# The output projection of a hybrid decoder layer: two row halves of 512 columns with the sample rows apart, in place of three blocks of 344

## What is computed

```
h = rmsnorm(x, g_mix);  z = h @ w_in
y = concat(dilated attention, banded attention) * silu(gates)
h = x + y @ w_out                                       # the stage that changes
out = rmsnorm(h + (p @ w_ple) * sigmoid(rmsnorm(h, g_ple) @ w_pg), g_final)
```

## Time and profile before

| | |
|---|---|
| median of 3 runs | 2786.28 us (2779.0 to 2786.41) |
| the profiled execution | 2782.93 us |
| its span in the profile | 2780.7 us |
| PE busy | 2574.9 us, 93% |
| DVE, ACT, POOL busy | 31%, 22%, 22% |
| mean granted clock of PE | 0.952 |

### The profile page before, as it was taken

One profiled execution on the slowest core, in us unless ns is written; L12 is line 12 of the kernel. 1 busy time (PEld: TensorE's weight loads), 2 busy tenths in 40 slices (PEclk: granted clock), 3 DMA queues, 4 the chain that ended last, 5 costly groups with the idle time before them and its releaser, 6 DMA issues.

```text
span 2780.7 us, 40810 instructions
## 1 busy us (share of the span) xinstructions
PE 2574.9 (93%) x16857; PEld 2394.1 (86%) x16857; DVE 856.3 (31%) x2130; ACT 610.4 (22%) x1458; POOL 618.7 (22%) x653
## 2 busy tenths in 40 slices
PE   4999999999999999999999988989999959999980
PEld 4998888888888898888888988879999949999980
DVE  7022322322322314444444213141101163233324
ACT  5022222222222213334544100020000030111113
POOL 2322222222222222211222222223333201111110
PEclk7999999999999999999999999899999979999995
DMA  4232222222222224434443343163222262322316
GB/s 165 65 111 86 84 87 85 88 84 88 88 84 88 69 81 117 123 113 136 129 129 113 117 134 97 56 194 92 81 80 84 73 192 84 93 85 83 93 54 240
DMA packets 301818, 287.96 MB, mean 104 GB/s; under 512 B 20721, under 2 KB 267305, under 8 KB 298281
## 3 DMA queue, kind: packets, MB, share of 16 engines
q1 hardware_dynamic: 278754, 241.11, 28.8%
q10 hardware_dynamic: 17856, 27.34, 2.8%
q0 software_dynamic: 5024, 16.92, 1.7%
HBM read 215.48 MB, written 69.81 MB: 103 GB/s over the span
## 4 chain that ended last, share of the span: by engine, by line
PE 84%; DVE 7%; DMA 5%; ACT 2%; issue 1%; POOL 1%; SPq 0%; POOLq 0%; DVEq 0%; ACTq 0%
PE psum L786 18%; PE psum L788 17%; PE psum L787 17%; PE psum L859 5%; PE psum L861 5%; PE psum L860 5%; PE psum L634 4%; PE psum L610 3%; PE psum L620 3%; PE psum L708 2%; PE psum L810 1%; PE psum L664 1%; DMA out<-f_out 1%; PE psum L689 1%; PE psum L675 1%
## 5 line engine op out<-in xcount | busy, mean ns | idle before, releaser
L786 PE MATMUL psum<-act_hi,w_hi 128*128 128x344 f32 x3264 | 1086.0, 333 | 14.4 <-DVE act_lo L1324 13.5
L788 PE MATMUL psum<-act_hi,w_lo 128*128 128x344 f32 x3264 | 1057.9, 324 | 0.0
L787 PE MATMUL psum<-act_lo,w_hi 128*128 128x344 f32 x3264 | 1057.9, 324 | 0.0
L786 PEld LDWEIGHTS psum<-act_hi,w_hi 128*128 128x128 f32 x3264 | 628.4, 193 | 35.4 <-issue 29.6
L787 PEld LDWEIGHTS psum<-act_lo,w_hi 128*128 128x128 f32 x3264 | 626.9, 192 | 0.0
L788 PEld LDWEIGHTS psum<-act_hi,w_lo 128*128 128x128 f32 x3264 | 626.8, 192 | 0.0
L567 POOL CAST w_hi<-w_raw 128x512 fp32r<-128x512 f32 x272 | 179.8, 661 | 1645.1 <-PE psum L788 1505.4
L569 POOL TENSOR_TENSOR w_lo<-w_raw,w_hi 128x512 fp32r<-128x512 f32 x272 | 366.2, 1346 | 21.8
L1135 DVE COPY prob_t<-psum 128x512 f32<-128x512 f32 (+2 forms) x96 | 53.4, 557 | 497.3 <-PE psum L634 490.8
L937 ACT ACTIVATE prob_t<-psum 128x512 f32<-128x512 f32 (+2 forms) x96 | 47.1, 491 | 420.5 <-PE psum L634 388.4
L859 PE MATMUL psum<-act_hi,u_even 128*128 128x344 f32 x384 | 125.7, 327 | 8.6 <-DVE u_even L1347 7.8
(11 more groups left out here) (190 smaller groups left out, 2742.4 us busy)
## 6 DMA issues: line engine op xcount, KB each, us to landing
w_raw<-in_w_in SPq DMA_DIRECT2D x208, 256.0 KB, 3.0
w_raw<-in_w_out SPq DMA_DIRECT2D x64, 256.0 KB, 2.8
u_raw<-in_w_pg SPq DMA_DIRECT2D x16, 1024.0 KB, 6.2
z_scratch<-stage ACTq DMA_DIRECT2D x72, 172.0 KB, 1.9
h_scratch<-h_row ACTq DMA_DIRECT2D x16, 516.0 KB, 3.3
h_stage<-h_scratch SPq DMA_DIRECT2D x16, 516.0 KB, 4.7
h_in<-h_scratch SPq DMA_DIRECT2D x48, 172.0 KB, 2.6
x_in<-in_x_prompt SPq DMA_DIRECT2D x8, 1024.0 KB, 5.3
```

The lines of the kernel that those rows point to most:

```text
L786: pe.matmul(psum[:, bank, 0:T3], w_hi[:, slot, x, :], act_hi[:, k, rows], start=(k == 0), stop=False, skip_group_check=True)
L787: pe.matmul(psum[:, bank, 0:T3], w_hi[:, slot, x, :], act_lo[:, k, rows], start=False, stop=False, skip_group_check=True)
L788: return pe.matmul(psum[:, bank, 0:T3], w_lo[:, slot, x, :], act_hi[:, k, rows], start=False, stop=stop, skip_group_check=True)
```

## The change

The rows of the output projection are cut into two halves of the prompt (512 columns each, a full PSUM bank) and the sample's 8 columns apart. A new tile `ys_both` holds the sample's high and low parts side by side (16 columns per k). For each k TensorE now runs `key_tile`: high weights by high and by low activations of half 0; high weights by all 16 sample columns at once; low weights by the high activations of half 0; low weights by the 8 high sample columns; then the three products of half 1. That is six matmuls of 512 columns, one of 16, one of 8; before, nine of 344. k is outermost for every tile, the wait on `h_bank_free` covers all banks of tile i-2 at once, and the wait on `s_split` comes first. The residual comes in four 128-row pieces for each half and one 8-row piece. x_cols is loaded by two DMAs. ACT copies two banks of 512; DVE adds the two sample parts from PSUM into `h_row` by a reduce, and waits for the store two tiles back before it writes.

```diff
+            ("ones", [P, P], F32), ("y_in", [P, 4, S], F32), ("ys_both", [P, KT, 2 * NB], F32R))
...
-                for t in range(2):
-                    q0 = T3 * t
-                    sp.dma_start(x_cols[:, par, 3 * t:3 * t + 2, :], ...)
-                    sp.dma_start(x_cols[0:88, par, 3 * t + 2, :], ...)
-                sp.dma_start(x_cols[:, par, 6:8, :], ...)
-                sp.dma_start(x_cols[0:80, par, 8, :], ...)
-                sp.dma_start(x_cols[80:88, par, 8, :], x_s[:, cols]) ...
+                sp.dma_start(x_cols[:, par, 0:8, :], x_p[:, cols].rearrange("(c p) n -> p c n", p=P)) ...
+                sp.dma_start(x_cols[0:NB, par, 8, :], x_s[:, cols]) ...
...
+            def key_tile(i, k):
+                slot, x = (WG * (NZ + i) + k // WG) % WRING, k % WG
+                b0, first, last = 3 * (i % 2), k == 0, k == KT - 1
+                hi_w, lo_w = w_hi[:, slot, x, :], w_lo[:, slot, x, :]
+                for t in range(2):
+                    rows = slice(512 * t, 512 * t + 512)
+                    pe.matmul(psum[:, b0 + t, :], hi_w, act_hi[:, k, rows], start=first, ...)
+                    pe.matmul(psum[:, b0 + t, :], hi_w, act_lo[:, k, rows], ...)
+                    if t == 0:
+                        pe.matmul(psum[:, b0 + 2, 0:2 * NB], hi_w, ys_both[:, k, :], start=first, ...)
+                    mm = pe.matmul(psum[:, b0 + t, :], lo_w, act_hi[:, k, rows], ...)
+                    if t == 0:
+                        pe.matmul(psum[:, b0 + 2, 0:NB], lo_w, ys_both[:, k, 0:NB], ...)
+                return mm
...
-            for i in range(1, KT):
-                for t in range(3):
-                    ...
-                    for k in range(KT):
-                        ...
-                        mm = three(bank, NZ + i, k, t, False)
-                    residual(i, t, bank)
+            for i in range(KT):
+                par = i % 2
+                if i >= 2:
+                    pe.wait_ge(sem("h_bank_free"), 3 * (i - 1))
+                for k in range(KT):
+                    if i == 0:
+                        pe.wait_ge(sem("y_split"), k + 1)
+                    if k % WG == 0:
+                        pe.wait_ge(sem("w_split"), WG * (NZ + i) + k // WG + 1)
+                    mm = key_tile(i, k)
+                    ...
+                pe.wait_ge(sem(f"xc_loaded{par}"), 32 * (i // 2 + 1))
+                for t in range(2):
+                    for x in range(4):
+                        mm = pe.matmul(psum[:, 3 * par + t, x * P:(x + 1) * P], x_cols[:, par, 4 * t + x, :], ident[:], ...)
+                    mm.then_inc(sem("h_produced"), 1)
+                pe.matmul(psum[:, 3 * par + 2, 0:NB], x_cols[0:NB, par, 8, :], ident[0:NB, 0:NB], ...).then_inc(sem("h_produced"), 1)
...
-                for t in range(3):
+                for t in range(2):
                     act.wait_ge(sem("h_produced"), 3 * i + t + 1)
-                    act.activation(h_row[:, par, T3 * t:T3 * (t + 1)], psum[:, 3 * par + t, 0:T3], ACT.Copy) ...
+                    act.activation(h_row[:, par, 512 * t:512 * t + 512], psum[:, 3 * par + t, :], ACT.Copy) ...
...
-            chain(dve.tensor_copy(act_hi[:, :, S:R], ystmp[:]))
-            dve.tensor_tensor(act_lo[:, :, S:R], ystmp[:], hi32[:, :, S:R], ALU.subtract) ...
+            chain(dve.tensor_copy(ys_both[:, :, 0:NB], ystmp[:]))
+            dve.tensor_tensor(ys_both[:, :, NB:], ystmp[:], ys_both[:, :, 0:NB].bitcast(F32), ALU.subtract) ...
...
             for i in range(KT):
+                dve.wait_ge(sem("h_produced"), 3 * i + 3)
+                if i >= 2:
+                    dve.wait_ge(sem(f"h_stored{i % 2}"), 16 * (i // 2))
+                both = psum[:, 3 * (i % 2) + 2, 0:2 * NB].rearrange("p (c n) -> p n c", c=2)
+                dve.tensor_reduce(h_row[:, i % 2, S:R], both, AX.X, ALU.add).then_inc(sem("h_bank_free"), 1)
                 dve.wait_ge(sem("h_bank_free"), 3 * i + 3)
```

More of the change, by code:

```diff
@@ L216, in build @@
         ysm = zs[:, 0:KT, :]
-        acc, h_row, sq, x_cols, ones, y_in = at(
+        acc, h_row, sq, x_cols, ones, y_in, ys_both = at(
             W_END, ("acc", [P, R], F32), ("h_row", [P, 2, R], F32), ("sq", [P, R], F32), ("x_cols", [P, 2, 9, P], F32),
-            ("ones", [P, P], F32), ("y_in", [P, 4, S], F32))
+            ("ones", [P, P], F32), ("y_in", [P, 4, S], F32), ("ys_both", [P, KT, 2 * NB], F32R))
         u_even, y_nat, h_in, gcol = at(0, ("u_even", [P, 2, KT + 2, P], F32R), ("y_nat", [P, 2, 3, P], F32), ("h_in", [P, 2, T3], F32),
@@ L481, in load_x_cols @@
                 cols = slice(i * P, i * P + P)
-                for t in range(2):
-                    q0 = T3 * t
[L484 to L488, removed]
+                sp.dma_start(x_cols[:, par, 0:8, :], x_p[:, cols].rearrange("(c p) n -> p c n", p=P)).then_inc(sem(f"xc_loaded{par}"), 16)
+                sp.dma_start(x_cols[0:NB, par, 8, :], x_s[:, cols]).then_inc(sem(f"xc_loaded{par}"), 16)
             sp.wait_ge(sem("ys_ready"), 1)
@@ L804, in _ @@
                         mm.then_inc(sem("w_used"), 1)
[L806 to L811, removed]
+            def key_tile(i, k):
[4 more added lines that the diff above has]
+                    rows = slice(512 * t, 512 * t + 512)
+                    pe.matmul(psum[:, b0 + t, :], hi_w, act_hi[:, k, rows], start=first, stop=False, skip_group_check=True)
+                    pe.matmul(psum[:, b0 + t, :], hi_w, act_lo[:, k, rows], start=False, stop=False, skip_group_check=True)
+                    if t == 0:
+                        pe.matmul(psum[:, b0 + 2, 0:2 * NB], hi_w, ys_both[:, k, :], start=first, stop=False, skip_group_check=True)
+                    mm = pe.matmul(psum[:, b0 + t, :], lo_w, act_hi[:, k, rows], start=False, stop=False, skip_group_check=True)
+                    if t == 0:
+                        pe.matmul(psum[:, b0 + 2, 0:NB], lo_w, ys_both[:, k, 0:NB], start=False, stop=False, skip_group_check=True)
+                return mm
@@ L813, in _ @@
             pe.wait_ge(sem("bank_free"), UNITS)
             pe.wait_ge(sem("ys_ready"), 1)
-            for k in range(KT):
[L816 to L820, removed]
-                for t in range(3):
-                    mm = three(t, NZ, k, t, False)
-                if k % WG == WG - 1 and k < KT - 1:
-                    mm.then_inc(sem("w_used"), 1)
@@ L825, in _ @@
-            for t in range(3):
-                residual(0, t, t)
-            for i in range(1, KT):
[L828 to L834, removed]
-                        mm = three(bank, NZ + i, k, t, False)
-                        if t == 2 and k % WG == WG - 1 and k < KT - 1:
-                            mm.then_inc(sem("w_used"), 1)
-                    residual(i, t, bank)
+            pe.wait_ge(sem("s_split"), 2)
@@ new lines, in _ @@
+            for i in range(KT):
[8 more added lines that the diff above has]
+                    mm = key_tile(i, k)
+                    if k % WG == WG - 1 and k < KT - 1:
+                        mm.then_inc(sem("w_used"), 1)
+                pe.wait_ge(sem(f"xc_loaded{par}"), 32 * (i // 2 + 1))
+                for t in range(2):
+                    for x in range(4):
+                        mm = pe.matmul(psum[:, 3 * par + t, x * P:(x + 1) * P], x_cols[:, par, 4 * t + x, :], ident[:], start=False, stop=(x == 3), skip_group_check=True)
+                    mm.then_inc(sem("h_produced"), 1)
+                pe.matmul(psum[:, 3 * par + 2, 0:NB], x_cols[0:NB, par, 8, :], ident[0:NB, 0:NB], start=False, stop=True, skip_group_check=True).then_inc(sem("h_produced"), 1)
@@ L1041, in _ @@
                     act.wait_ge(sem("h_squared"), i - 1)
-                for t in range(3):
+                for t in range(2):
                     act.wait_ge(sem("h_produced"), 3 * i + t + 1)
-                    act.activation(h_row[:, par, T3 * t:T3 * (t + 1)], psum[:, 3 * par + t, 0:T3], ACT.Copy).then_inc(sem("h_bank_free"), 1)
+                    act.activation(h_row[:, par, 512 * t:512 * t + 512], psum[:, 3 * par + t, :], ACT.Copy).then_inc(sem("h_bank_free"), 1)
                 act.wait_ge(sem("h_bank_free"), 3 * i + 3)
@@ L1319, in _ @@
             dve.wait_ge(sem("produced"), UNITS)
-            chain(dve.tensor_copy(act_hi[:, :, S:R], ystmp[:]))
-            dve.tensor_tensor(act_lo[:, :, S:R], ystmp[:], hi32[:, :, S:R], ALU.subtract).then_inc(sem("s_split"), 2)
+            chain(dve.tensor_copy(ys_both[:, :, 0:NB], ystmp[:]))
+            dve.tensor_tensor(ys_both[:, :, NB:], ystmp[:], ys_both[:, :, 0:NB].bitcast(F32), ALU.subtract).then_inc(sem("s_split"), 2)
             for k in range(KT):
```

## The result

The changed kernel takes **2840.68 us** (median of 4 runs, 2835.63 to 2844.27) against 2785.53 for the kernel before: 1.0202 of it, 95% interval 1.018 to 1.0224. It is slower by 55 us where 41 were forecast, and lies 0.7 us above the range of 2804 to 2840. In a second set of runs (experiment 7) it took 2833.48 (2830.28 to 2840.32), 1.0182 of before (1.015 to 1.0213). That this median lies inside the range says little: the whole moves by some 10 us with what lies outside the stage, and the stage itself was 12 us off in both.

A forecast was written before the change was run, and what follows sets the result against it. The prediction took TensorE's matmul rate to bound the output projection after tile 0. It added 40.8 + 0.2 = +41.0 us to the profiled 2782.9, giving 2823.9 us, range 2804 to 2840.

The forecast's parts named there:

- What bounds the stage: Output projection: for 15 of 16 tiles bound only by TensorE's matmul rate, never idle over 371.1 us, clock 1.00.
- the clock's rival: Output projection: TensorE's granted clock falls to 1.2 GHz for a tenth of the k, +34 us more, 2858; chance 0.06.
- Order and banks: Output projection: k outermost and one wait for all three banks of tile i-2, met some 20 us early; no cost.
- weights, x_cols and the DVE sum: Output projection: POOL's weight split, fewer x_cols DMA issues and DVE's sample sum change nothing, within half a microsecond.
- The small matmul: Output projection, 16 or 8 columns: each costs the uncovered weight load behind it, 110 ns, 220 for each k.
- Both rivals with a hidden load: Load behind a small matmul hidden, 20 ns each: 2761 without long ones' fixed part, chance 0.04; 2780.5 with it, 0.03.
- A 512-column matmul: Output projection's long products: 512 / 2.4 plus a fixed 13.4 ns, 226.7 ns each; six are 1360 ns.
- overhead by column: Long matmuls' excess grows with columns, 233.2 ns for 512: a k of 1619 ns, +50.2 us, 2833.3.
- The old k: Output projection before: nine 344-column matmuls at 156.7 ns, 1410 ns for each k.
- The residual: Residual matmuls of each tile: 18 records cost 2.0 us in either version; change zero, bounds 0.1 us a tile.
- Tile 0: Output projection's first tile: supply-bound, longer k hidden in PE's waits, no backlog, only the last k exposed: +0.2 us.
- 40.8: Output projection, tiles after the first: each k 1580 ns, 170 more than 1410, over 15 x 16 = 240: +40.8 us.

The follow-up runs named there:

- experiment 7: The changed kernel run once more, unaltered: 2833.48 us, 1.0182 of the kernel before.
- experiment 5: The kernel before, still 344 columns, with k outermost for all tiles and one wait for the three banks: 2783.57 us against 2781.5, 1.0006.
- 1: The changed kernel without both small matmuls for k = 1 to 15: 2786.56 us, 1.0016 of the kernel before.
- 9: The kernel before with one 16-column matmul added for each k of tiles 1 to 15, into a spare bank: 2811.92 us, 1.0097 of before.
- 4: The changed kernel with the 16-column matmul moved between the two long ones using the same high weights: 2836.24 us, 1.019 of the kernel before.
- 3: The changed kernel with each small matmul replaced by one of 236 columns for k = 1 to 15: 2835.91 us, 1.0193 of the kernel before.
- experiment 8: The changed kernel with sample columns stationary and weights streaming past, once in four k, for k = 1 to 15: 2815.74 us, 1.0108 of the kernel before.
- experiment 6: The changed kernel with eight runs of single-kind matmuls added twice behind TensorE's last work: 512 columns took 234.0 ns in float32r, 215.7 in bfloat16.
- experiment 2: The changed kernel with the sample's residual matmul on all 128 rows, zero-padded, instead of 8: 2833.79 us, 1.018 of the kernel before.

## Why the prediction was right in kind and short in size
The windows of tiles 1 to 15 hold 240 k and the residuals of 16 tiles less 0.1 to 0.3 us of the last. With 2.01 us for a residual before and 2.29 after (2012.37 - 2010.08, the start of its first matmul, a long step after the load at 2009.85), a k is (371.25 - 31.9) / 240 = 1414 ns before and (424.31 - 36.4) / 240 = 1616 after. The steps between weight loads, averaged over the same windows, give 1414 and 1616 too. That is the check that counts, since the terms below are taken from these windows and would add up to them in part by themselves. By the prediction's own steps:

- **What bounds the stage: right.** TensorE's rate of matmuls alone, before and after; no wait appeared on PE in tiles 1 to 15 and the clock stayed at 1.00 (the clock's rival fell). Order and banks cost nothing (experiment 5); weights, x_cols and the DVE sum left PE waiting nowhere in 424.31 us.
- **The small matmul: right.** Taken at 110 ns, measured 108 in the changed kernel, 111 and 113 by taking out and putting in (experiments 1 and 9). Both rivals with a hidden load are out: a repeat is paid (4), 220 free columns fit under a load (3), and only a shorter load makes it cheaper (8).
The Trainium skill (TensorE: Matmul & The Clock Gate, "Wait — 56ns, not 53.3ns?") has a floor of about 25 ns between starts however few the columns. Matmuls of 16 columns on 128 weight columns start 108 to 112 ns apart, and even the short steps of experiment 8 are about 60 ns, so it binds in no run here.
- **A 512-column matmul: the step that failed.** "What is beyond the columns is fixed there. I take 226.7". It is 233: (1616 - 217) / 6, the prediction's own upper bound, "overhead by column", of 233.2. What is beyond the columns is not fixed: the 13 to 14 ns at 344 columns grow to 20 or 21 at 512, nearly in proportion (experiment 6). The argument for a fixed part was borrowed from another data type, plain float32, at two cycles a column, and from mean durations of rows, of which the prediction itself says that they are no price. That is 39 ns a k, **9.4 us**. The old k was 1414 and not 1410, which takes back 0.9, the small ones at 217 for 220 another 0.7.
- **The residual: failed too.** "Zero; the bounds are a transition more or less, 0.1 us a tile." It was 0.28 us a tile, **4.4 us** over the window, because the 8-row piece changes the rows of the array in use, twice (experiment 2). Blocks of 88 rows before had cost no such step, and I took 8 for more of the same.
- **Tile 0: the step was wrong, its price can't be told.** The prediction says that "no backlog is carried on". In the changed kernel one is: PE was never idle after the first k, and the last low part and the first residual matmul stand
```profile
1864.39 1.23 DVE L1323 TENSOR_TENSOR act_lo<-y_in,act_hi 128x1024 fp32r<-128x1024 f32 x1 [0.26 <-ACT act_hi L1034]
1869.31 0.94 PE L835 MATMUL psum<-ident,x_cols 128*128 128x128 f32 x7
```
3.7 us apart (1869.31 - 1865.62), 3.4 and 2.1 in experiments 7 and 6, where tile 0 is the same; before it was 1.6, and 1.6 again in 5 and 9. But how long the supply takes differs more than that. From the first issue of y_in to the residual, tile 0 took 34.5, 35.7 and 35.8 us with the old code (before, 5, 9) and 35.8, 35.0 and 35.9 with the new one (changed, 7, 6). So the 1.3 us between the two profiles is within what the same code does twice.

Together 40.8 + 9.4 - 0.9 - 0.7 + 4.4 = 53.0 of the 53.1 us in tiles 1 to 15. The other 2 of the 55 us between the medians lie in tile 0 and outside the stage, where runs of the same code differ by more; no run here assigns them.

Can this split win? Six long ones cost 1399 ns, the old k 1414: 15 ns are left for 24 sample columns, and the cheapest way tried (8) took about 130. No version tried wins. Inside the three blocks of 344 the sample's 24 columns cost an estimated 11 ns (24 of 1032 columns at 157.1 / 344 ns each).

## What to carry to other kernels
Price a matmul as the larger of its own stream and the weight load of the one behind it: with 128 weight columns of four bytes that load was 108 ns, so anything under about 236 float32r columns cost the same. Splitting equal work unevenly lost here even with fewer instructions: three blocks of 344 are better than 512 + 512 + 8. Read the price from the starts of the weight loads, not from the starts of matmul rows, and a rate for a data type only from rows of that type.

## What was new
- float32r matmuls stream slower than the full clock gives: 234.0, 157.4 and 119.1 ns for 512, 344 and 256 columns with every other engine and all DMAs silent, while bfloat16 takes 215.7 for 512. At the halved clock the 344 columns had no excess. What sets the limit at the full clock, no run here tells.
- A matmul on 8 of the 128 rows behind one on all rows costs about 0.29 us more than one padded to 128 with zeros, both sides counted.
- The same stage took 424.31 us in two executions that differ by 14 us as a whole.
